# Experts' weights laid tile by tile in memory, and the rows of the experts spread by two passes over high and low parts

## The reference

```python
# x: 256 x 1024; router: 1024 x 8; gate, up: 8 x 1024 x 3584; down: 8 x 3584 x 1024
logits = x @ router                       # the best 2 of 8 experts for each token
weight = softmax over the chosen 2
out = sum over experts e of  weight[:, e] * ((silu(x @ gate[e]) * (x @ up[e])) @ down[e])
h = layer_norm(ALPHA * h + out)
```

## Time and profile before

| what | value |
|---|---|
| median of 3 runs | 3247.16 us |
| profiled execution | 3250.54 us, its span 3248.7 us |
| experts' stage (first gather to last spread added) | 2177.6 to 3237 us of the span |
| TensorE busy in the span | 3092.7 us, 95% |
| VectorE, ScalarE busy | 2298.4 us, 71%; 1757.2 us, 54% |
| memory read | 693.73 MB, mean 214 GB/s |
| DMA share in the experts' stage | 0.94, 333 GB/s |

### The profile page before, as it was taken

How to read it: one execution, slowest core, us unless ns; L and a number is a source line. 1 busy time by engine, 2 the same in 40 slices (tenths; PEclk the granted TensorE clock), 3 DMA queues, 4 the chain that set the end, 5 groups by cost and what they waited for, 6 DMA issues and landing times.

```text
span 3248.7 us, 38581 instructions
## 1 busy us (share of the span) xinstructions
PE 3092.7 (95%) x15010; PEld 2526.1 (78%) x15010; DVE 2298.4 (71%) x2134; ACT 1757.2 (54%) x1647; POOL 46.1 (1%) x28
## 2 busy tenths in 40 slices
PE   8999999999998999999989999979999999999998
PEld 6777887877887787777878877767787787877876
DVE  7886556886556556765455667658887887887888
ACT  4564445465444444553334445536676676766765
POOL 0000000100000000000000000000000000000000
PEclk9999999999999999999999999989999999999999
DMA  6434555434555454335554543339998998999997
GB/s 242 143 130 145 187 183 175 159 117 135 183 185 188 157 169 156 130 112 180 189 168 157 181 154 123 113 118 339 334 362 304 350 354 302 358 338 312 364 327 266
DMA packets 351081, 697.25 MB, mean 215 GB/s; under 512 B 12225, under 2 KB 17217, under 8 KB 350785
## 3 DMA queue, kind: packets, MB, share of 16 engines
q1 hardware_dynamic: 347024, 687.75, 61.8%
q10 hardware_dynamic: 3888, 7.07, 0.7%
HBM read 693.73 MB, written 1.05 MB: 214 GB/s over the span
## 4 chain that ended last, share of the span: by engine, by line
PE 75%; DVE 10%; DMA 5%; ACT 4%; DVEq 3%; issue 3%; PEld 0%; ACTq 0%; POOL 0%; PEldq 0%; SPq 0%
PE banks L641 22%; PE banks L643 21%; PE banks L642 21%; DVE weights_low L1594 4%; ACT weights_high L1194 2%; DMA weights_raw<-in_moe_w_down_dram 2%; PE banks L796 1%; DMA weights_raw<-in_moe_w_up_dram 1%; DMA weights_raw<-in_moe_w_gate_dram 1%; PE banks L678 1%; PE banks L1106 1%; PE banks L1121 1%; PE banks L753 1%; ACT weights_transposed L1373 1%; PE banks L782 1%
## 5 line engine op out<-in xcount | busy, mean ns | idle before, releaser
L1594 DVE TENSOR_TENSOR weights_low<-weights_raw,weights_high 128x2048 fp32r<-128x2048 f32 (+1 forms) x658 | 1490.7, 2269 | 532.5 <-ACT weights_high L1194 526.8
L1194 ACT ACTIVATE weights_high<-weights_raw 128x2048 fp32r<-128x2048 f32 (+1 forms) x658 | 1247.7, 1898 | 578.4 <-PE banks L643 454.2
L641 PE MATMUL banks<-weights_high,h_transposed_high 128*128 128x512 f32 x2784 | 1122.6, 403 | 28.7 <-DVE weights_low L1594 15.3
L643 PE MATMUL banks<-weights_high,h_transposed_low 128*128 128x512 f32 x2784 | 1087.9, 391 | 11.5 <-issue 11.5
L642 PE MATMUL banks<-weights_low,h_transposed_high 128*128 128x512 f32 x2784 | 1086.0, 390 | 0.0
L641 PEld LDWEIGHTS banks<-weights_high,h_transposed_high 128*128 128x128 f32 x2784 | 527.5, 189 | 163.4 <-issue 23.5
L643 PEld LDWEIGHTS banks<-weights_high,h_transposed_low 128*128 128x128 f32 x2784 | 526.9, 189 | 123.8 <-issue 12.8
L642 PEld LDWEIGHTS banks<-weights_low,h_transposed_high 128*128 128x128 f32 x2784 | 527.9, 190 | 109.4 <-issue 8.6
L641 PE MATMUL banks<-weights_high,y_transposed_high 128*128 128x512 f32 x1096 | 433.5, 396 | 9.1 <-DVE y_transposed_low L2446 4.6
L643 PE MATMUL banks<-weights_high,y_transposed_low 128*128 128x512 f32 x1096 | 427.2, 390 | 0.0
L642 PE MATMUL banks<-weights_low,y_transposed_high 128*128 128x512 f32 x1096 | 427.0, 390 | 0.0
(11 more groups left out here) (308 smaller groups left out, 2068.2 us busy)
## 6 DMA issues: line engine op xcount, KB each, us to landing
weights_raw<-in_w_in_dram SPq DMA_DIRECT2D x152, 1024.0 KB, 5.0
weights_raw<-in_moe_w_gate_dram SPq DMA_DIRECT2D x114, 1024.0 KB, 6.6
weights_raw<-in_moe_w_up_dram SPq DMA_DIRECT2D x112, 1024.0 KB, 6.5
weights_raw<-in_moe_w_down_dram SPq DMA_DIRECT2D x112, 1024.0 KB, 6.4
weights_raw<-in_w_up_dram SPq DMA_DIRECT2D x32, 1024.0 KB, 5.6
weights_raw<-in_w_down_dram SPq DMA_DIRECT2D x32, 1024.0 KB, 5.0
weights_raw<-in_ffn_w_gate_dram SPq DMA_DIRECT2D x10, 1024.0 KB, 5.1
weights_raw<-in_ffn_w_up_dram SPq DMA_DIRECT2D x10, 1024.0 KB, 5.1
```

What stands on the lines that cost most here:

```text
L641: nc.tensor.matmul(out_of[t], lhs(0, k, t), high[:, k], start=begin, stop=False)
L643: mm = nc.tensor.matmul(out_of[t], lhs(1, k, t), high[:, k], start=False, stop=end)
L1194: nc.scalar.activation(tile_view(WH, h % SPLIT, tile), tile_view(raw, h % RAW, tile), ACT.Copy).then_inc(high_ready, 1)
L1594: v.tensor_tensor(tile_view(WL, h % SPLIT, tile), tile_view(raw, h % RAW, tile), tile_view(WH, h % SPLIT, tile).bitcast(F32), ALU.subtract ...
```

## The change

Three things change, all around the experts' stage.

1. The three expert weights are laid in device memory tile by tile before launch (`tile_by_tile`), so that a tile is one run of 1 MB, and each partition's share of it one run of 8 KB. The load takes them as 128 runs of 8 KB in place of 512 of 2 KB. All other weights stay as they were.
2. The experts' outputs `YE` become two float32r tensors, high (ScalarE's copy) and low (a new VectorE subtraction). `CHOICET` is float32r too, in one part, since it now holds only zeros and ones. A spread is two float32r MATMULs, high and low. The buffers move to unused halves of `h_transposed` and `y_transposed`.
3. The token's weight is applied when a spread is added: `scalar_tensor_tensor` (bank times weight plus `MERGED`) in place of `tensor_tensor`. `CHOICEW` and its two instructions in `choose` are gone. The zeroing of `YE` and `CHOICET` moves from the route stage to the head of the experts' stage, as three multiplications of `MERGED` by zero.

```diff
+def tile_by_tile(w):
+    n, e, rows, cols = w.shape
+    return (w.reshape(n, e, rows // (KT * P), KT, P, cols // NB, NB).transpose(0, 1, 2, 5, 4, 3, 6)
+            .reshape(n, e, rows // (KT * P), cols // NB, P, TILE))
...
-        YE = PRf[:, 4096:5120].rearrange("p (b c) -> p b c", b=2)
+        YE = [h.rearrange("p k s -> p (k s)")[:, 1024:2048].rearrange("p (b c) -> p b c", b=2) for h in HT]
@@ SyncE, load
-                        src = a[tile["name"]][tile["layer"], bass.ds(expert, 1), tile["row"]:tile["row"] + tile["rows"] * P,
-                                              tile["col"]:tile["col"] + tile["width"]].rearrange("e (k p) c -> p (e k) c", p=P)
+                        src = a[tile["name"]][tile["layer"], bass.ds(expert, 1), tile["row"] // (KT * P),
+                                              tile["col"] // NB].rearrange("e p c -> p (e c)")
@@ TensorE, spread
-                    nc.tensor.matmul(PS[:, bank, :], CHOICET[:, half, s // 2, :], YE[:, s % 2, :], start=True,
+                    nc.tensor.matmul(PS[:, bank, :], CHOICET[:, half, s // 2, :], YE[0][:, s % 2, :], start=True, stop=False)
+                    nc.tensor.matmul(PS[:, bank, :], CHOICET[:, half, s // 2, :], YE[1][:, s % 2, :], start=False,
                                      stop=True).then_inc(spread_full, 1)
@@ VectorE, route
-                v.memset(YE, 0.0)
-                v.memset(CHOICET[:, 1], 0.0)
@@ VectorE, head of experts
+                for part in YE:
+                    v.tensor_scalar(part.rearrange("p b c -> p (b c)"), MERGED[:, 0], 0.0, None, ALU.mult)
+                v.tensor_scalar(CHOICET[:, 1].rearrange("p t s -> p (t s)"), MERGED[:, 0, 0:T * P], 0.0, None, ALU.mult)
+                dve.drain().then_inc(down_read, 1)
@@ VectorE, choose
-                    dve.drain()
-                    for t in range(T):
-                        v.tensor_scalar(CHOICEW[:, t], CHOICE[:, t], ROUTE[:, t, 2, bass.ds(at, 1)], None, ALU.mult)
@@ VectorE, spread
-                    v.tensor_tensor(acc, acc, PS[:, bank], ALU.add).then_inc(spread_read, 1)
+                    last = (m + T * N_EXPERTS - 1) % (T * N_EXPERTS)
+                    v.scalar_tensor_tensor(out=acc, in0=PS[:, bank], scalar=ROUTE[:, s // 2, 2, bass.ds(last, 1)], in1=acc,
+                                           op0=ALU.mult, op1=ALU.add).then_inc(spread_read, 1)
@@ VectorE, end of an expert
+                        dve.wait_ge(down_high, m + 1)
+                        v.tensor_tensor(YE[1].rearrange("p b c -> p (b c)"), PS[:, 6:8].rearrange("p b c -> p (b c)"),
+                                        YE[0].rearrange("p b c -> p (b c)").bitcast(F32), ALU.subtract).then_inc(down_read, 1)
```

More of the change, by code:

```diff
@@ L368, in build @@
         XG = [h.rearrange("p k s -> p (k s)")[:, 0:1024].rearrange("p (k s) -> p k s", k=KD) for h in HT]
-        YE = PRf[:, 4096:5120].rearrange("p (b c) -> p b c", b=2)
+        YE = [h.rearrange("p k s -> p (k s)")[:, 1024:2048].rearrange("p (b c) -> p b c", b=2) for h in HT]
         CHOICE = PRf[:, 5120:5376].rearrange("p (t s) -> p t s", t=T)
-        CHOICEW = PRf[:, 5376:5632].rearrange("p (t s) -> p t s", t=T)
-        CHOICET = PRf[:, 5632:6144].rearrange("p (b t s) -> p b t s", b=2, t=T)
+        CHOICET = YT[0].rearrange("p k s -> p (k s)")[:, 1024:1536].rearrange("p (b t s) -> p b t s", b=2, t=T)
         index_roped = sem("index_keys_roped")
@@ L439, in build @@
         hid_turned = sem("hidden_turned")
+        down_high = sem("down_high_ready")
         down_read = sem("down_read")
@@ L607, in load @@
                         tile = st["tiles"][h % (PAIR // 2)]
-                        src = a[tile["name"]][tile["layer"], bass.ds(expert, 1), tile["row"]:tile["row"] + tile["rows"] * P,
-                                              tile["col"]:tile["col"] + tile["width"]].rearrange("e (k p) c -> p (e k) c", p=P)
+                        src = a[tile["name"]][tile["layer"], bass.ds(expert, 1), tile["row"] // (KT * P),
+                                              tile["col"] // NB].rearrange("e p c -> p (e c)")
                         sp.wait_ge(low_ready, STATIC + h - RAW + 1 + done)
-                        sp.dma_start(tile_view(raw, (STATIC + h) % RAW, tile), src).then_inc(landed[(STATIC + h) % RAW], 16)
+                        sp.dma_start(raw[:, (STATIC + h) % RAW], src).then_inc(landed[(STATIC + h) % RAW], 16)
                     for h in range(SPLIT - 1):
@@ L1113, in turn_choice @@
                     for t in range(T):
-                        tr = nc.tensor.transpose(PS[:, bank, t * P:(t + 1) * P], CHOICEW[:, t, :], ident)
+                        tr = nc.tensor.transpose(PS[:, bank, t * P:(t + 1) * P], CHOICE[:, t, :], ident)
                     tr.then_inc(choice_turned, 1)
@@ L1531, in experts @@
             def experts(st):
-                act.drain().then_inc(down_read, 1)
                 def gather(m, kk, bank=5):
@@ L1570, in experts @@
                         act.wait_ge(tile_used, i * PAIR + STATIC + (half + 1) * (PAIR // 2))
-                        nc.scalar.activation(YE.rearrange("p b c -> p (b c)"), PS[:, 6:8].rearrange("p b c -> p (b c)"),
-                                             ACT.Copy).then_inc(down_read, 1)
+                        nc.scalar.activation(YE[0].rearrange("p b c -> p (b c)"), PS[:, 6:8].rearrange("p b c -> p (b c)"),
+                                             ACT.Copy).then_inc(down_high, 1)
             run = dict(setup=setup, product=product, pairs=pairs, index=index,
@@ L2496 @@
                 positions=np.asarray(inputs["positions"]).reshape(T, P).T)
+    for name in ("moe_w_gate_2", "moe_w_up_2", "moe_w_down_2"):
+        laid[name] = tile_by_tile(np.asarray(inputs[name]))
     for name in _INS + ["shape_constants", "parameters"]:
```

## The result

The changed kernel takes 3234.96 us (median of 7 runs, 3231.09 to 3237.97) against 3247.34 us before (7 runs, 3244.12 to 3258.28). The ratio is 0.9949 with a 95% interval of 0.9934 to 0.9964, so 12 to 21 us less; the medians are 12.4 us apart. It is faster, and inside the range of 3209 to 3237 us, but 27.6 us were forecast. The profiled execution has a span of 3236.2 us against 3248.7, 12.5 us less, and this difference can be laid out piece by piece.

What follows compares the result with a forecast made beforehand. TensorE was taken to pace the experts' stage, loads close behind. Spread 12.8, choose 5.4, loads 10 and head 0.1 less tail 0.7 made 27.6 us saved: 3220 us, forecast stretch 3213 to 3227 (chance 0.55), range 3209 to 3237.

Steps and rivals of the forecast that it cites:

- packets' size is no matter: Rival, expert loads: 2 KB and 8 KB packets move alike, so 3230 to 3238 us; chance 0.22.
- The spread: TensorE: two float32r MATMULs, 0.46 us, replace one fp32 MATMUL of 0.86 us; 32 spreads gain 12.8 us.
- `choose`: VectorE before tile 10's low part: without the second pair each stall shrinks 0.68 us; eight gain 5.4 us.
- The loads: Expert weight loads: 8 KB packets take away most of TensorE's waits for late loads; gain 10 us, bounds 0 and 12.5.
- The packets' rate: Expert weight loads: 8 KB packets at 420 GB/s take 2.50 us a tile in place of 2.72.
- The stalls' worth: TensorE's waits not explained by tile 10's stalls: at most 12.5 us to win from faster loads.
- The fourth rival, slow packets: Expert loads: 8 KB packets may take 0.41 us each, 3.3 us a tile, making 3311 us; chance 0.06.
- My rival of the ring: Load, high, low, next load set the pace of four tiles, so gains are waited away: about 3242 us; chance 0.07.
- The turns: Three loop turns: a later branch on VectorE could delay tile 2's low part; cost 0, bound 6 us.
- The fused add: VectorE, adding a spread with the token's weight: 0.68 us, as the plain add takes, so free.
- Head and tail: Experts' stage ends: head -0.1 us as multiplications replace MEMSETs; tail +0.7 us as the subtraction delays the last adds.
- The subtraction: VectorE before tile 2's low part: 1.23 us, covered by ScalarE's copy and rounding; cost 0, uncovered 10 us.

Runs made afterwards that it cites:

- e10: e9 with choose after an expert's tile 9, zeroing behind the stage's first choose, and the last high spreads before YE's low part; 3192.34 us, ratio 0.9838.
- e9: The changed kernel with six raw slots and the four expert pairs written out, without loop turns between them; 3197.58 us, ratio 0.9851 to the kernel before.
- e3: Load test computing nothing of the reference: 2 KB and 8 KB runs, two or four in flight, then four slots with ScalarE and VectorE rounding; 935.93 us.
- e6: The changed kernel with six raw slots in the experts' stage, two more than before; 3221.15 us, ratio 0.9925 to the kernel before.
- e1: The kernel before with only the experts' weights laid tile by tile and loaded in 8 KB runs; 3251.03 us, ratio 0.9995.
- e12: The kernel before (row order, 2 KB, old spread and choose) with six raw slots; 3235.20 us, ratio 0.9969.
- e2: The changed kernel with the experts' weights back in row order, loaded in 2 KB runs; 3236.27 us, ratio 0.9950 to the kernel before.
- e11: The changed kernel with e4's layout (2 KB runs) and six raw slots; 3218.45 us, ratio 0.9917 to the kernel before.
- e5: Load test computing nothing of the reference: four loads in flight, 2 KB or 8 KB runs, alone or beside working engines; 1233.98 us.
- e4: The changed kernel with each tile one 1 MB run in memory, but loaded as 512 runs of 2 KB; 3247.74 us, ratio 0.9985 to the kernel before.

## Why the prediction was right in sign and wrong in size

The time lies in the range of 3209 to 3237 us only because the range took in most of the rival "packets' size is no matter" (3230 to 3238). The forecast's own stretch, 3213 to 3227, missed it by 8 us. Of the 15 us that are missing in the profiled execution, the loads are 10.5.

**The spread: right.** 12.8 us forecast, 13.1 measured. The price came from starts of one fp32 spread and of float32r products, and both held.

**`choose`: right.** 0.68 us a stall, 5.4 us, to the tenth. The high part was there, as its absence from VectorE's waits had said. In e10 the rest of that stall is gone too (from start to start 3.8 us in e9, nothing in e10).

**The loads: the step that failed.** A gain of 10 us was forecast, a loss of 0.5 measured. Three things stood in that step. The packets' rate (2.50 us a tile) was right for a full queue, as e3 measured; in the stage a load's packets took 2.81 us. The stalls' worth, up to 12.5 us, was right, as e6 showed by taking them away (8 to 14 us). Wrong was what ties them: "the loads' slack grows from 0.04 to 0.26 us a tile, so a delay is made up in 4 tiles". That holds for a queue with four loads always in flight. Here a load is issued only when its slot is free, and on average 2.1 loads are in flight. e3 shows with nothing else at work that such a ring takes 2.78 us a tile in 8 KB packets and 2.73 in 2 KB ones: the slack that was counted on is not there. I sorted the 330 loads of the stage by their lead, that is by how long before the previous load's landing they were issued, and took the distance of their landings:

| lead | before: loads, mean distance | after: loads, mean distance |
|---|---|---|
| under 2.0 us | 53, 4.25 us | 49, 3.91 us |
| 2.0 to 2.7 | 21, 2.91 | 33, 3.09 |
| 2.7 to 3.4 | 41, 3.04 | 49, 3.24 |
| 3.4 to 4.1 | 110, 2.96 | 83, 3.11 |
| over 4.1 | 105, 2.77 | 116, 2.62 |

Only the loads with a lead over 4.1 us land closer than before, among those that can be compared; with leads of 2.0 to 4.1 us the 8 KB loads land further apart. (Under 2.0 us the leads differ too much among themselves.) The rival "the packets' size is no matter" is the one that came true in its number of 3230 to 3238, but not for its reasons: neither a rule of line rate nor memory's own rate (e3 parts the sizes, 381 and 414 GB/s), but the ring. The fourth rival, slow packets, had a part of the mechanism: single 8 KB packets are slow, but 4% of them take over 0.7 us, where it had priced all at 0.41 us. My rival of the ring was asked whether the ring sets the mean pace, and was right to be rejected for that; I did not ask whether the ring keeps single delays alive.

**The turns: a cost where 0 was taken.** 3.1 us, inside the bound of 6 but not by its mechanism: the low part of tile 2 was not waited for. TensorE's own standstill at one turn was 0.8 us longer, and 11 more MATMULs ran at 1.2 GHz. The other kernels with three turns do not bear out that this comes from the change: from e1 to e12 TensorE stood still for 11.8 to 13.0 us in the three, and 24 to 38 MATMULs ran at 1.2 GHz (24 in e2, which has all of the change but the layout; 38 in e11). So the 3.1 us may be chance from execution to execution.

**The fused add: not quite free.** 0.746 us, not the 0.68 of the like forms in the earlier trace rows; why was not tried. TensorE's weight loads for spreads waited 3.3 us in ten for it, and of this some 0.8 us reached the MATMULs.

**Head and tail: right.** The head's own part is -0.2 us (forecast -0.1). That the first gather is 1.5 us later in the trace comes from the stage before, which ended 1.7 us later. The tail is +0.9 us (forecast +0.7); TensorE's clock did not fall in its pause of 2.75 us, the spreads' MATMULs stand 0.23 us apart, and the adds, 2.73 us for four, set the end.

**The subtraction: hidden, as predicted**, but for the tail: no new wait for the low part of tile 2 has appeared (the one at the stage's first expert stands in both traces).

## What to carry to other kernels

Before you price a faster transfer, look at what issues it: if loads wait for a slot, count how many are in flight and how much lead the late ones have, because the rate of a full queue says little of a ring that waits for its slots. Measure the load with the ring closed, as e3's last phases do, and not only the queue. A delay in a ring of four slots came back every fourth tile; look for that period in the waits, and try one or two more slots before another layout. Where a trace shows an engine standing still for nothing ("issue") at a loop's turn, price the low clock behind it too.

## What was not expected of the hardware

- A load of 1 MB that is issued into an empty queue takes 5.0 to 5.3 us from issue to landing in 2 KB packets and 4.7 to 5.0 us in 8 KB packets (first loads of the phases of e3 and e5). With two in flight a tile takes 2.88 or 2.55 us, with four 2.71 or 2.49. A packet's median is 84 ns at 2 KB and 309 ns at 8 KB in the experts' stage; 2% of the latter take 980 ns and more, 2% of the former 186 ns and more.
- In a ring of four slots, closed by ScalarE and VectorE, 8 KB packets lengthen from 314 to 337 ns on average and 2 KB packets do not (e3).
- 1 MB tiles in one piece of memory, read in 2 KB packets, load slower in the kernel than the same packets at a distance of 4 to 14 KB: 157 us of waits against 114 in e2. This costs 11 us with four slots and nothing with six.
- A turn of this loop costs TensorE 3.7 to 4.5 us of standing still, and then 7 to 14 MATMULs at 1.2 GHz (before and after).

Open: why single loads among the engines' traffic are slow; what makes single 8 KB packets slow, and so why with leads of 2 to 4 us the 8 KB loads land further apart than the 2 KB ones, though e3 with two in flight has them faster; why e4's addresses are slower; and why TensorE's standstill differs from turn to turn.
